# Prompt attention: probabilities times values as f32r products, with the high and low halves of the values side by side, and the probabilities scaled on GpSimd

## What is computed

```python
v = jnp.einsum('btc,chd->bthd', c_kv, w_uv)              # values from the 256-wide latent rows
s = jnp.einsum('bqhd,bkhd->bhqk', qn, k_nope) + jnp.einsum('bqhr,bkr->bhqk', qr, k_rope)
p = jax.nn.softmax(jnp.where(mask, s * SOFTMAX_SCALE, -jnp.inf), axis=-1)   # causal, 128 queries at a time
o = jnp.einsum('bhqk,bkhd->bqhd', p, v)
```

## Time and profile before

| | us |
|---|---|
| median of 3 runs (2008.62 to 2016.44) | 2015.69 |
| profiled execution | 2021.29 |
| its span, first to last instruction | 2019.5 |
| prompt attention in it | 178.2 to 311.4 |
| mean granted TensorE clock | 0.986 |

### The profile page before, as it was taken

The page is one execution under the profiler, slowest core; times in us unless marked ns, Lnnn a source line. Parts: engine busy times, 40 slices in busy tenths (PEclk is TensorE's granted clock), DMA queues, the critical chain, the costliest instruction groups (busy, mean ns, idle before and its releaser), DMA issues.

```text
span 2019.5 us, 36447 instructions
## 1 busy us (share of the span) xinstructions
PE 1955.5 (97%) x13333; PEld 1874.8 (93%) x13333; DVE 1050.2 (52%) x1877; ACT 754.5 (37%) x1525; POOL 688.1 (34%) x679
## 2 busy tenths in 40 slices
PE   7989999999999999999999999999989999999998
PEld 7877658999999999999999999999989999999997
DVE  3566764655565555556325425427854852542542
ACT  4444654555555555332112212246653221221220
POOL 2220002432232224253333333355545433333331
PEclk9998999999999999999999999999989999999999
DMA  5321001111111110222222222232222222222222
GB/s 144 63 63 35 22 3 34 39 42 37 39 33 42 40 38 19 67 75 84 84 84 81 76 83 83 83 102 66 72 57 79 83 84 83 82 76 81 83 84 77
DMA packets 251863, 131.48 MB, mean 65 GB/s; under 512 B 43009, under 2 KB 249538, under 8 KB 251666
## 3 DMA queue, kind: packets, MB, share of 16 engines
q1 hardware_dynamic: 251666, 129.68, 23.0%
q10 hardware_dynamic: 76, 0.18, 0.0%
HBM read 126.21 MB, written 3.61 MB: 64 GB/s over the span
## 4 chain that ended last, share of the span: by engine, by line
PE 87%; DVE 8%; issue 2%; ACT 2%; DMA 1%; DVEq 0%; POOL 0%; ACTq 0%; POOLq 0%
PE ps L200 18%; PE ps L203 18%; PE ps L201 18%; PE ps L1187 7%; PE ps L1189 7%; PE ps L1188 7%; PE ps L1215 3%; PE ps L998 2%; PE ps L973 2%; PE ps L1154 1%; PE ps L229 1%; DVE arena L1819 1%; PE ps L989 1%; DVE arena L2065 1%; PE ps L1196 0%
## 5 line engine op out<-in xcount | busy, mean ns | idle before, releaser
L200 PE MATMUL ps<-split,whi 128*128 128x288 f32 x3024 | 863.5, 299 | 12.2 <-DVE arena L733 4.8
L201 PE MATMUL ps<-split,whi 128*128 128x288 f32 x3024 | 853.9, 296 | 0.0
L194 POOL TENSOR_TENSOR wlo<-raw,whi 128x1024 fp32r<-128x1024 f32 x188 | 456.8, 2431 | 668.6 <-ACT whi L171 668.5
L203 PE MATMUL ps<-split,wlo 128*128 128x288 f32 x3024 | 658.2, 298 | 0.0
L200 PEld LDWEIGHTS ps<-split,whi 128*128 128x128 f32 x3024 | 573.4, 190 | 15.9 <-issue 14.1
L201 PEld LDWEIGHTS ps<-split,whi 128*128 128x128 f32 x3024 | 574.6, 190 | 0.7
L203 PEld LDWEIGHTS ps<-split,wlo 128*128 128x128 f32 x3024 | 489.7, 189 | 0.0
L171 ACT CAST whi<-raw 128x1024 fp32r<-128x1024 f32 x187 | 194.7, 1042 | 406.5 <-DMA raw<-in_ffn_w_up 242.1
L1187 PE MATMUL ps<-split,split 128*128 128x384 f32 x768 | 268.4, 350 | 0.2 <-DVE arena L1274 0.2
L1189 PE MATMUL ps<-split,split 128*128 128x384 f32 x768 | 258.1, 336 | 0.0
L1188 PE MATMUL ps<-split,split 128*128 128x384 f32 x768 | 257.4, 335 | 0.0
(11 more groups left out here) (269 smaller groups left out, 2134.6 us busy)
## 6 DMA issues: line engine op xcount, KB each, us to landing
raw<-in_ffn_w_up SPq DMA_DIRECT2D x96, 512.0 KB, 3.8
raw<-in_ffn_w_down SPq DMA_DIRECT2D x48, 512.0 KB, 3.9
arena<-in_cache_ckv SPq DMA_DIRECT2D x128, 128.0 KB, 2.0
raw<-in_rec_w_in SPq DMA_DIRECT2D x16, 512.0 KB, 3.9
raw<-in_attn_w_o SPq DMA_DIRECT2D x8, 512.0 KB, 3.9
raw<-in_rec_w_out SPq DMA_DIRECT2D x8, 512.0 KB, 3.9
raw<-in_attn_w_down SPq DMA_DIRECT2D x7, 512.0 KB, 8.8
raw<-in_attn_w_uq SPq DMA_DIRECT2D x48, 64.0 KB, 2.2
```

The lines of the kernel that those rows point to most:

```text
L194: pool.tensor_tensor(wlo[:, t % RING, :], raw[:, t % RING, :], f32(whi[:, t % RING, :]), ALU.subtract).then_inc(w_lo, 1)
L200: pe.matmul(o, wh, a, start=first, stop=False)
L201: pe.matmul(o, wh, b, start=False, stop=False)
L203: mm = pe.matmul(o, wl, a, start=False, stop=last)
```

## The change

- The values are kept twice. `vals` becomes four f32r tensors (128 tokens each) with, for every head, 64 columns of high part and 64 of low part side by side. ScalarE writes the high part of all eight blocks (`value_high`), VectorE the low part of all eight (`value_low`).
- The transposed probabilities are kept twice as well, ten 128x128 pieces a head, two heads interleaved in 20 places: ScalarE's copy writes the high part `pT_hi`, a new VectorE subtraction `prob_low` the low part `pT_lo`. VectorE does it in step u for unit u - 4, between the maximum and the reciprocal.
- `attend` issues for each of the four key blocks an f32r product of 128-wide weights (high | low) with the high probabilities, and a 64-wide one (high) with the low probabilities. The result has two halves, in partitions 0 to 63 and 64 to 127: ScalarE copies the upper one to SBUF (`half_kept`), VectorE adds it to the lower one into `oT` (`outputs`), for each head.
- The scaling of the probabilities moves from VectorE to GpSimd (`prompt_pool`).
- Places: `kcat` moves to the constants' cosine and sine tables and to `ckv`; `pT_lo`, one probability buffer and `o_half` lie in the ring of weight tiles. So the four output-projection tiles are loaded later, between page loads of the second running sequence, and the rope copies into the last two `kcat` places come after the value blocks.
- The waits follow: banks 2 and 3 are handed back by `prob_low` instead of the copy, bank 6 after every head.

```diff
-        qs = area(A_P + 2048, NH, TN)
+        qs = area(A_P + 4608, NH, TN)
...
-        vals = area(A_V, 4, D)
+        vals = [area(at + k * 2 * D, NH, 2 * DV, dt=F32R) for at in (A_V, A_P) for k in range(2)]
...
-        V_ACT = [0, 1, 4, 5]
...
-                pe.wait_ge(v_act, 2)
+                pe.wait_ge(v_dve, 2)
...
-                pe.wait_ge(v_act, 4)
+                pe.wait_ge(v_dve, 6)
             elif j == 2:
-                pe.wait_ge(v_dve, 4)
+                pe.wait_ge(v_dve, 8)
...
-            pe.wait_ge(v_dve, 2)
+            pe.wait_ge(v_dve, 4)
...
-        def value_kept(eng, copy, i, s):
-            eng.wait_ge(v_ps, i + 1)
-            copy(vals[:, i // 2, (i % 2) * 512:(i % 2 + 1) * 512], ps[:, V_BANK[i], :]).then_inc(s, 1)
+        def value_half(i, low):
+            return vals[i // 2][:, 8 * (i % 2):8 * (i % 2) + 8, DV * low:DV * low + DV]
+        def value_high(act, i):
+            act.wait_ge(v_ps, i + 1)
+            act.copy(value_half(i, 0), ps[:, V_BANK[i], :].rearrange("p (h e) -> p h e", e=DV)).then_inc(v_act, 1)
+        def value_low(dve, i):
+            dve.wait_ge(v_act, i + 1)
+            dve.tensor_tensor(value_half(i, 1), ps[:, V_BANK[i], :].rearrange("p (h e) -> p h e", e=DV),
+                              f32(value_half(i, 0)), ALU.subtract).then_inc(v_dve, 1)
...
-            value_kept(dve, dve.tensor_copy, 2, v_dve)
-            value_kept(dve, dve.tensor_copy, 3, v_dve)
-            for k in range(4):
-                ins = dve.tensor_copy(kcat[DN:DN + DR, k, :], krw_rope[:, :])
-            ins.then_inc(k_rope, 1)
+            for i in range(4):
+                value_low(dve, i)
+            for k in range(2):
+                dve.tensor_copy(kcat[k][DN:DN + DR, :], krw_rope[:, :])
             key_norm(dve, 0)
-            value_kept(dve, dve.tensor_copy, 6, v_dve)
-            value_kept(dve, dve.tensor_copy, 7, v_dve)
+            for i in range(4, 8):
+                value_low(dve, i)
...
+            for k in range(2, 4):
+                ins = dve.tensor_copy(kcat[k][DN:DN + DR, :], krw_rope[:, :])
+            ins.then_inc(k_rope, 1)
...
-            value_kept(act, act.copy, 0, v_act)
-            value_kept(act, act.copy, 1, v_act)
+            for i in range(4):
+                value_high(act, i)
...
-            value_kept(act, act.copy, 4, v_act)
-            value_kept(act, act.copy, 5, v_act)
+            for i in range(4, 8):
+                value_high(act, i)
...
-        pT = area(A_P, 2, 4, TP)
-        kcat = area(A_P + 4096, 4, T)
-        pr = [area(A_P + 4096 + 2304, 512), area(A_P + 4096 + 2304 + 512, 512), sq[1], rs[1]]
+        pT_hi = area(A_P + 4096, 20, P, dt=F32R)
+        pT_lo = nc.alloc_sbuf_tensor_at("pT_lo", [P, 20, P], F32R, offset=raw_at)
+        kcat = [cst[:, C_COS + k * T:C_COS + (k + 1) * T] for k in range(2)] + [ckv[:, k, :] for k in range(2)]
+        pr = [area(A_P + 6656, 512), raw[:, 2, 512:1024], sq[1], rs[1]]
...
+        o_half = raw[0:DV, 3, 0:512]
+        p_tlo = sem("p_tlo")
...
-            pe.matmul(ps[:, u % 2, 0:n], qc[0:96, h, qb * P:(qb + 1) * P], kcat[0:96, h % 4, 0:n],
+            pe.matmul(ps[:, u % 2, 0:n], qc[0:96, h, qb * P:(qb + 1) * P], kcat[h % 4][0:96, 0:n],
...
         def new_scores(pe, h):
...
-            pe.matmul(ps[0:TN, 7, (h % 8) * TN:(h % 8 + 1) * TN], kcat[0:96, h % 4, TP:T], qc[0:96, h, TP:T],
+            pe.matmul(ps[0:TN, 7, (h % 8) * TN:(h % 8 + 1) * TN], kcat[h % 4][0:96, TP:T], qc[0:96, h, TP:T],
                       start=True, stop=True).then_inc(p_n, 1)
         def probs_turn(pe, u):
...
-                pe.wait_ge(p_tev, u - 1)
+                pe.wait_ge(p_tlo, u - 1)
             for kb in range(qb + 1):
-                mm = pe.transpose(ps[:, 2 + u % 2, kb * P:(kb + 1) * P], pr[u % 4][:, kb * P:(kb + 1) * P], ident)
+                at = qb - kb if u // 4 % 2 else kb
+                mm = pe.transpose(ps[:, 2 + u % 2, at * P:(at + 1) * P], pr[u % 4][:, kb * P:(kb + 1) * P], ident)
             mm.then_inc(p_t, 1)
+        def turned(v, u):
+            h, qb = divmod(u, 4)
+            if h % 2:
+                return v[:, 5 * (3 - qb):5 * (3 - qb) + 6 * qb + 1:6, :]
+            return v[:, qb + 1:qb + 1 + 5 * qb + 1:5, :]
+        def queries(v, h, kb):
+            at = 5 * (3 - kb) if h % 2 else 5 * kb + kb + 1
+            return v[:, at:at + 4 - kb, :].rearrange("p a q -> p (a q)")
         def attend(pe, h):
-            if h >= 2 and h % 2 == 0:
-                pe.wait_ge(p_oev, h // 2)
-            pe.wait_ge(p_tev, 4 * h + 4)
-            r = slice(DV * (h % 2), DV * (h % 2) + DV)
+            if h >= 1:
+                pe.wait_ge(p_oev, 2 * h)
+            pe.wait_ge(p_tlo, 4 * h + 4)
             for kb in range(4):
-                mm = pe.matmul(ps[r, 6, kb * P:TP], vals[:, kb, h * DV:(h + 1) * DV], pT[:, h % 2, kb, kb * P:TP],
-                               start=(kb == 0), stop=(kb == 3))
+                mm = pe.matmul(ps[:, 6, kb * P:TP], vals[kb][:, h, :], queries(pT_hi, h, kb), start=(kb == 0),
+                               stop=(kb == 3))
+                if kb == 0:
+                    for c in range(4):
+                        pe.matmul(ps[0:DV, 6, c * P:TP], vals[c][:, h, 0:DV], queries(pT_lo, h, c), start=False,
+                                  stop=False)
...
+                if u >= 11 and u % 4 == 3:
+                    half_kept(act, (u - 11) // 4)
...
-                    act.copy(pT[:, h % 2, 0:qb + 1, qb * P:(qb + 1) * P],
-                             ps[:, 2 + v % 2, 0:(qb + 1) * P].rearrange("p (k q) -> p k q", q=P)).then_inc(p_tev, 1)
+                    act.copy(turned(pT_hi, v), ps[:, 2 + v % 2, 0:(qb + 1) * P].rearrange("p (k q) -> p k q", q=P))\
+                       .then_inc(p_tev, 1)
+            for h in range(NH - 2, NH):
+                half_kept(act, h)
+        def prob_low(dve, v):
+            h, qb = divmod(v, 4)
+            dve.wait_ge(p_tev, v + 1)
+            dve.tensor_tensor(turned(pT_lo, v), ps[:, 2 + v % 2, 0:(qb + 1) * P].rearrange("p (k q) -> p k q", q=P),
+                              f32(turned(pT_hi, v)), ALU.subtract).then_inc(p_tlo, 1)
+        def prompt_pool(pool):
+            for v in range(UNITS):
+                m = (v % 4 + 1) * P
+                pool.wait_ge(p_inv, v + 1)
+                pool.tensor_scalar(pr[v % 4][:, 0:m], pr[v % 4][:, 0:m], cols[:, 8 + v % 4:9 + v % 4], None,
+                                   ALU.mult).then_inc(p_ok, 1)
         def prompt_dve(dve):
-            for u in range(UNITS + 1):
+            for u in range(UNITS + LAG + 1):
...
-                if u >= 1:
+                if u > LAG:
+                    prob_low(dve, u - LAG - 1)
+                if 1 <= u <= UNITS:
                     v = u - 1
-                    m = (v % 4 + 1) * P
                     dve.wait_ge(p_exp, v + 1)
+                    if v >= 4:
+                        dve.wait_ge(p_ok, v - 3)
                     dve.reciprocal(cols[:, 8 + v % 4:9 + v % 4], cols[:, 4 + v % 4:5 + v % 4]).then_inc(p_inv, 1)
-                    dve.wait_ge(p_inv, v + 1)
-                    dve.tensor_scalar(pr[v % 4][:, 0:m], pr[v % 4][:, 0:m], cols[:, 8 + v % 4:9 + v % 4], None,
-                                      ALU.mult).then_inc(p_ok, 1)
+                if u >= 12 and u % 4 == 0:
+                    outputs(dve, u // 4 - 3)
...
-                    if u % 8 == 7 and u >= 15:
-                        outputs(dve, u // 8 - 1)
...
-            outputs(dve, 7)
-        def outputs(dve, j):
-            dve.wait_ge(p_o, 2 * j + 2)
-            if j == 0:
+            for h in range(NH - 2, NH):
+                outputs(dve, h)
+        def outputs(dve, h):
+            dve.wait_ge(p_oev, 2 * h + 1)
+            if h == 0:
                 dve.wait_ge(s_onat, 64)
-            dve.tensor_copy(oT[:, j, 0:TP], ps[:, 6, :]).then_inc(p_oev, 1)
+            dve.tensor_tensor(oT[DV * (h % 2):DV * (h % 2) + DV, h // 2, 0:TP], ps[0:DV, 6, :], o_half,
+                              ALU.add).then_inc(p_oev, 1)
+        def half_kept(act, h):
+            act.wait_ge(p_o, h + 1)
+            if h:
+                act.wait_ge(p_oev, 2 * h)
+            act.copy(o_half, ps[DV:2 * DV, 6, :]).then_inc(p_oev, 1)
...
+                    if b and i % 4 == 3:
+                        if i == 3:
+                            sp.wait_ge(p_o, NH)
+                        load_tile(sp, WO0 + i // 4, wo(i // 4))
...
-            for d in range(4):
-                load_tile(sp, WO0 + d, wo(d))
             down_store(sp)
-            sample_sp(sp)
+            sample_sp(sp, wo)
...
+            prompt_pool(pool)
```

10 lines of the change are left out of this document (5 added, 5 removed).

## The result

The changed kernel takes 2028.50 us in the median of 7 runs (2018.74 to 2032.21), the kernel before 2016.44 us beside it (7 runs, 2008.62 to 2024.44): a ratio of 1.0062, 95% interval 1.0035 to 1.0089. It is slower by 12 us, where 3.4 us less were forecast, and outside the stated range, which ended at 2025 us.

The account below looks back on a forecast made before the run. TensorE was taken to bound the changed stage, prompt attention. Terms 0.6 + 1.0 - 5.1 - 1.2 + 0.8 + 0.5 = -3.4 us, against the median 2015.7, gave 2012.3 us; range 2000 to 2025.

Parts of the forecast that it names:

- six pairs at -0.85 us each: Steady pairs of heads in prompt attention: 15.46 us falls to 14.6 after new waits, -5.1 us in all.
- first pair: First two heads of prompt attention: the key norm, already waited for, comes later through the same queue, +1.0 us.
- The products: Products of values and probabilities: 2.30 us per head become 1.2 in f32r, a gain of 1.1 us per head.
- GpSimd's price: Scaling of probabilities on GpSimd: 0.65 us for 384 and 0.8 for 512 columns, upper ends 1.0 and 1.3.
- Rival D: GpSimd scaling too slow: each us beyond 1.15 costs one per head, 2029.1 us at 2.2; chance 0.07.
- The layout of the key-sum half: Half pair with the key sum, laid out by hand: next 512-column scores at 6.7 us, losing 0.45 of the gain.
- The half with the key products: Other half of each pair: TensorE waits 0.9 us for the late key norm, plus some 0.1 us of waits.
- Mask additions: Eight additions on VectorE at unit 32 lose the cover of long products and delay the next maximum: +0.8 us.
- The tail: Last 512-column scores to last output copy: products halve but bank 6 changes hands per head, -0.5 us taken.
- Rival C: Waits make TensorE's clock fall once per pair in the loop for 3 to 5 us: 2024 to 2030 us; chance 0.1.
- Start: Before the first scores: absorbed queries wait for the low half of value block 5, +0.6 us.
- Moved loads: Output-projection weight loads between page loads of the second sequence: 0 us, at most 16 us if the cover failed.

Follow-up runs that it names:

- e7: Changed kernel with the kept half behind ScalarE's copy and, on VectorE, reciprocal, then key norm, then low part: ratio 1.0015, pair 14.42 us.
- e4: The changed kernel again, unedited, against the kernel before: ratio 1.0043, median 2025.51 us.
- e1: Changed kernel with GpSimd scaling only the first 128 columns of each unit, the rest left unscaled: ratio 1.0055 to the kernel before, pair 15.35 us.
- e5: Changed kernel with VectorE's key norm ahead of the low part of unit 2: ratio 1.0024 to the kernel before, pair 15.18 us.
- e11: e7 with the last head's products in bank 1 and the second block of new scores two units later on VectorE: ratio 0.9982.
- e2: Changed kernel with the scaling back on VectorE behind the reciprocal: ratio 1.0106 to the kernel before, pair 16.79 us.
- e9: The kernel before, unchanged, measured again: ratio 1.0006, pair 15.46 us.
- e3: Kernel before with only the scaling of the probabilities moved to GpSimd: ratio 1.0021, pair 15.84 us.
- e10: Kernel before with only the four output-weight loads moved between page loads of the second sequence: ratio 1.0017, pair 15.46 us.
- e12: The same kernel as e10, measured once more: ratio 1.0002 to the kernel before, pair 15.46 us.
- e13: The same kernel as e11, measured once more: ratio 0.9992 to the kernel before, pair 14.53 us.

## Why the prediction failed, step by step

The gain was to come from six pairs at -0.85 us each. That is the step that failed: a pair came out at +0.1 us (15.57 against 15.46). The layout lost 1.45 us of the 2.2 that TensorE gives up to waits; measured, all of the 2.0 went, and e7 gives 1.1 us back by the order of instructions on ScalarE and VectorE alone. The start and the tail were mis-sized besides. In the profiles of after and e4, against before and from the last value product to the last sample product, the terms of the sum came out so (us):

| term | forecast | after | e4 |
|---|---|---|---|
| start, last value product to first scores | +0.6 | +2.2 | +1.7 |
| first pair | +1.0 | +0.75 | -0.1 |
| six further pairs, mask additions with them | -4.3 | +2.6 | +1.3 |
| last pair, to its last 512-column scores | -1.2 | +0.1 | +0.1 |
| tail to the last output addition | -0.5 | +1.5 | +1.5 |
| from there to the first sample product | 0 | -0.4 | -0.4 |
| sample products at the lower clock | +1.0 | +2.4 | +2.2 |
| sum | -3.4 | +9.1 | +6.3 |

- **The products (right).** 1.2 us a head were forecast; from their start to the next scores it is 1.3 us, where the earlier trace rows have 2.30. The gain is 1.0 a head for the 1.1 booked.
- **GpSimd's price (wrong, and little of the miss).** 0.65 and 0.8 us were taken, 1.3 was the outer bound; the scaling takes 1.24 us for 384 and 1.57 for 512 columns. The choice of the nearest row (a cast) misled. Rival D put its turning point at 1.35 us, and the price is past it, but D's size was wrong as well: it counted each us beyond once per head. With 0.60 us (e1), the key-sum half gets 0.37 us back and the other one loses 0.14 to 0.24, so the pair gets 0.2; and with the order of e7 TensorE waits for GpSimd nowhere in the steady pairs, at the full price.
- **The layout of the key-sum half (failed here).** It let the low part of unit 0 end at 3.7 and the scaling of unit 3 begin at 3.9; they were at 3.9 and 4.06, the scaling ended at 5.62 and not 4.7, and the half took 7.40, not 6.7 us. Some 0.4 of the 0.7 is GpSimd's price (e1: 7.03). The rest came from single prices a tenth short along one chain: kept half (from 2.70, 0.58 long, laid out as 2.6 to 3.1), copy, low part, reciprocal, scaling. That this chain needn't be there at all is what the layout didn't ask: with the order of e7 and GpSimd at its full 1.57 us the half takes 6.70.
- **The half with the key products (failed).** It had 0.9 us of wait for the keys and 0.1 of others: 7.9 us. Measured 8.17: 0.53 for the keys, 0.39 more for the scaling; and the norm, which ended 2.0 us after the 512-column scores had begun (2.4 forecast), stands ahead of their maximum: it starts 1.95 us after them (224.63), in the other half 1.17 (216.45), and exponential, reciprocal and scaling are late with it. The layout followed the norm to the keys and not to what else is queued behind it. e5 takes the wait away: 7.80.
- **Mask additions (right).** +0.8 forecast; the pair with unit 32 takes 16.53 us, 0.97 over its neighbours. Both orders leave it (15.23 against 14.42).
- **The tail (wrong).** Laid out, it would be 11.2 us at the full clock and 13.3 at the lower one, taken 12.4; it was 14.4, over both. The last two heads' products begin 6.4 us after the last 512-column scores, where it was 5.8, and from there to the end of the last output addition it takes 7.9 us, where it was 7.1. The second head had to wait for the first one's kept half and addition (311.86, 1.39 us idle), at the lower clock on top. The handing over was in the layout; its 6.4 to about 4 us for the products was not reached. e7 to e11 gives 4.0 us back here.
- **Rival C (came true, but elsewhere).** The loop's clock stays at 1.00 in the steady pairs with waits of 1.7 us in 15.57. It was low ahead of the first scores and into the first pair (172.9 to 183.9), once more from 193 to 197 in this profile and not in e4, and at the end for 17 us instead of "3 to 5". The price goes into the start, into the tail and into the sample products. e1 and e2, with longer pairs or halves, show single falls of 3.4 us in the loop.
- **Start (the wait right, the clock left out).** +0.6 forecast for the absorbed queries; they begin after 0.84 us of idle time for the low part of a value block. When the first scores start scatters by 5 us between profiles (176.3 to 181.4), but the distance from the last value product does not: 7.7 to 7.8 us in before, e9 and e3, 8.4 in e10 and e12, 9.3 to 10.1 in the ten profiles with the new products. Beyond the wait, the absorbed queries themselves take up to 1.3 us longer (8.3 against 7.0), more of them lying at the lower clock. The forecast had the clock as a rival in the loop and as a cost at the end, not here.
- **Moved loads.** Booked at nothing; by their totals e10 and e12 don't contradict it, up to the 3 us above.

What the start, the stage and the sample products explain is 6 to 9 us. The two medians of the changed kernel (19 runs) lie 12 and 8 us over the kernel before. The rest of 2 to 3 us is in no stage that the profiles separate, and e11 and e13 show one of 1 to 2.5 us as well: 8 us less in the stage, 2 more at the start and 1.6 more in the sample products make 4.5 us, and the totals gain 3.2 and 2.0. The moved loads (e10, e12) don't account for it with any certainty, and the stretch behind, which no edit touches, scatters by 12 us between profiles. Where the rest goes remains open, and a rest of this size is not far from the scatter.

## What to carry to other kernels

Where the bounding engine is relieved and no engine becomes full, as here, the order in each engine's own list can take back the whole gain: lay out one period by hand, and for each instruction that waits ask what is queued behind it, all of it. An instruction that only hands a buffer on (here the kept half) belongs behind one that starts the next chain. And look at the stage's start and end apart: here several engines handed one bank to and fro, TensorE rested, its clock was low for 17 us, and the next stage paid 2.4 us too.

## What was not expected of the hardware

The scaling on GpSimd takes 0.60, 0.92, 1.24 and 1.57 us for 128, 256, 384 and 512 f32 columns, so 0.28 us and 0.32 more for each 128. The Trainium skill, "GPSIMD Engine Reference", section Performance versus the Vector engine, gives 769 ns measured for 512 elements in its best loop. The trace has twice that for this instruction, and the measurement decides.

Beside VectorE's key norm, which reads two SBUF tensors, single scalings take 0.49 us longer, whatever their own length. The first row is from e1's group (its maximum), the others are from the changed kernel's timeline:

```profile
L1091 POOL TENSOR_SCALAR raw<-raw,cols x16: 602/604/1089, 184.9 to 300.9; 128x128 f32<-128x128 f32 x16
```

```profile
222.96 1.75 DVE L973 SCALAR_TENSOR_TENSOR arena<-work,smallg 64x576 f32<-64x576 f32 x2
223.14 1.41 POOL L1091 TENSOR_SCALAR raw<-raw,cols 128x256 f32<-128x256 f32 x1 [1.65 <-DVE cols L1111]
```

So 0.60 became 1.09 us and 0.92 became 1.41, while the norm's two instructions went from 1.64 (e7, where they don't meet) to 1.75. The Trainium skill, "SBUF — State Buffer", section SBUF: two separate sides, says that the two engines share a port pair, held for a whole instruction when VectorE has two SBUF inputs. The trace agrees in part: the fixed 0.49 us fits a scaling that waits for the end of the norm's first instruction, but the second one then ran from 223.77 to 224.71, beside the scaling (to 224.55), and took 0.94 us where it takes about 0.8 alone; that it was shut out for the scaling's whole length isn't what these rows show.

TensorE's time at the lower clock differs from profile to profile of one kernel (at the stage's end 6.8 and 3.4 us in the kernel before), and it shows in the next stage only where it reaches into it: sample products of 500.1 to 500.3 us where it ended before them, 501.7 to 502.8 where it did not.
